# A two-layer hybrid trunk step: norm and projection of each tile right behind its combination, and a last norm split between ScalarE and VectorE

## What is computed

```python
for l in range(2):
    h = x * (1 + sc_a) + sh_a
    qa, ka, va, oa, ia, fa, qb, kb, vb, qc, kc, vc = split_proj(h @ w_in[l])
    ya, yb, yc = mlstm(...), windowed_attention(...), neighbourhood_attention(...)
    x = post_norm(x, concat(ya, yb, yc) @ w_out[l], g_a, ln_g[l, 0], ln_b[l, 0])
    h = x * (1 + sc_f) + sh_f
    x = post_norm(x, moe_ffn(h, ...), g_f, ln_g[l, 1], ln_b[l, 1])

def post_norm(x, y, gate, g, b):
    u = ALPHA * x + gate * y
    mu = mean(u); var = mean((u - mu) ** 2)
    return (u - mu) * rsqrt(var + 1e-5) * g + b
```

## Time and profile before

| | us |
|---|---|
| median of 3 runs | 1696.19 (1695.11 to 1696.98) |
| the profiled execution, its own time | 1693.52 |
| its span | 1691.7 |
| TensorE busy | 1452.2 (86%) |
| VectorE busy | 625.5 (37%) |
| ScalarE busy | 344.0 (20%) |
| GpSimd busy | 404.6 (24%) |
| mean granted clock of TensorE, of full speed | 0.925 |

### The profile page before, as it was taken

The page is one execution under the profiler, slowest core; times in us unless marked ns, Lnnn a source line. Parts: engine busy times, 40 slices in busy tenths (PEclk is TensorE's granted clock), DMA queues, the critical chain, the costliest instruction groups (busy, mean ns, idle before and its releaser), DMA issues.

```text
span 1691.7 us, 23077 instructions
## 1 busy us (share of the span) xinstructions
PE 1452.2 (86%) x8501; PEld 998.0 (59%) x8501; DVE 625.5 (37%) x1470; ACT 344.0 (20%) x886; POOL 404.6 (24%) x541
## 2 busy tenths in 40 slices
PE   6999999997993899987699999999679479899772
PEld 4888998665882333332378988967468433334220
DVE  2201332864467121111520133376537732122127
ACT  2111112653010111110231111156401011111001
POOL 1000043522623112111110002352265221112113
PEclk8999999999995999998899999999799679899886
DMA  9311103775129899997512111275130779999951
GB/s 368 97 60 60 58 33 108 270 261 215 41 90 360 360 372 419 410 397 292 231 45 67 56 61 55 71 259 213 40 123 38 322 290 382 418 396 419 400 205 62
DMA packets 75758, 356.26 MB, mean 211 GB/s; under 512 B 21152, under 2 KB 24480, under 8 KB 40832
## 3 DMA queue, kind: packets, MB, share of 16 engines
q1 hardware_dynamic: 41184, 291.58, 43.8%
q0 software_dynamic: 21888, 48.83, 8.2%
q10 hardware_dynamic: 12576, 14.37, 2.5%
HBM read 344.37 MB, written 33.12 MB: 223 GB/s over the span
## 4 chain that ended last, share of the span: by engine, by line
PE 67%; DMA 19%; DVE 8%; issue 2%; POOL 2%; ACT 1%; SPq 1%; ACTq 0%; POOLq 0%; DVEq 0%
PE bank L974 24%; DMA att<-h_rows,cur 11%; PE bank L1317 11%; PE bank L1202 7%; PE bank L1336 4%; DMA ring<-in_w_exp 3%; PE bank L1301 2%; PE bank L723 2%; PE bank L1128 2%; DMA att<-bias_full 2%; PE bank L1102 1%; DMA z<-in_w_ada 1%; PE bank L931 1%; PE bank L738 1%; PE bank L1224 1%
## 5 line engine op out<-in xcount | busy, mean ns | idle before, releaser
L974 PE MATMUL bank<-ring,hT 128*128 128x256 f32 (+1 forms) x1920 | 411.3, 374 | 8.4 <-ACT hT L1441 4.4
L974 PEld LDWEIGHTS bank<-ring,hT 128*128 128x128 f32 x1920 | 353.3, 191 | 53.9 <-issue 9.4
L1317 PE MATMUL bank<-ring,att 128*64 128x512 f32 (+1 forms) x448 | 188.4, 653 | 3.7 <-DMA z<-in_w_exp 3.7
L1317 PE MATMUL bank<-z,att 128*64 128x512 f32 (+1 forms) x416 | 167.2, 626 | 16.6 <-DMA ring<-in_w_exp 16.6
L1202 PE MATMUL bank<-ring,hT 128*128 128x256 f32 x640 | 145.2, 386 | 7.1 <-DMA ring<-in_w_out 5.6
L1202 PEld LDWEIGHTS bank<-ring,hT 128*128 128x128 f32 x640 | 122.6, 194 | 23.9 <-issue 7.3
L2339 DVE TENSOR_TENSOR att<-att,bank 128x256 f32<-128x256 f32 x38 | 16.0, 421 | 295.4 <-ACT att L1671 295.4
L1317 PEld LDWEIGHTS bank<-ring,att 128*64 128x64 f32 (+1 forms) x448 | 61.2, 164 | 84.4 <-issue 82.6
L1317 PEld LDWEIGHTS bank<-z,att 128*64 128x64 f32 (+1 forms) x416 | 53.1, 152 | 76.2 <-issue 76.2
L2621 POOL COPY cur<-att 128x1 int32<-128x1 int32 (+1 forms) x38 | 6.9, 182 | 379.7 <-ACT att L1678 280.9
L1301 PE MATMUL bank<-const,att 128*128 128x128 f32 x320 | 48.5, 301 | 54.7 <-DMA att<-h_rows,cur 54.6
(11 more groups left out here) (362 smaller groups left out, 2185.3 us busy)
## 6 DMA issues: line engine op xcount, KB each, us to landing
...
```

The lines of the kernel that those rows point to most:

```text
L974: last = eng.matmul(bk[:, i * UN:i * UN + nw], hTv[:, k, t * P:(t + 1) * P], w[:, k, 0:nw], start=(k == 0), stop=(k == KD - 1))
L1317: last = eng.matmul(bank[2 + j][c * m_:(c + 1) * m_, :], e["xT"][:, j, k * P + c * m_:k * P + (c + 1) * m_], wv[c][:, :, k, :], start=(k = ...
```

## The change

Between the layers, TensorE's order changes. Tile 0 is turned behind tile 2's combination, as before; tiles 3 and 4 are combined before tile 1 is turned; tiles 2, 3 and 4 are turned each behind the projection of one tile, and the waits for the copied-out banks are taken tile by tile instead of piece by piece. ScalarE norms and copies strictly tile by tile (before, the norms ran two tiles ahead), and the second half of tile 3, like that of tile 4, is copied out by VectorE. On VectorE, `ln_nm` of the previous tile stands between the two halves of a combination instead of behind the statistics.

At the end, ScalarE does the statistics of every tile: a copy of the tile with a running sum, the sum times -1/1024 (minus the mean), the square of x minus the mean with a running sum, and that times 1/1024 plus 1e-5. The copies' outputs go to a place nobody reads. GpSimd still raises to -0.5. VectorE does scale and shift of every tile with two 1024-wide scalar-tensor-tensor operations, (x - mean) * ln_g and the result * root + ln_b, two tiles behind its combinations. GpSimd's `ln_shift` is gone there.

The diff, without the line that names the new steps for the semaphores:

```diff
@@ -313,6 +313,10 @@
 
         n = self.n - 1
         return self.ev.event(f"bank_full{n % BANKS}", ("full", n))
+
+    def fill(self, ins, *key):
+
+        ins.then_inc(*self.filled_as(*key))
 
     def filled_as(self, *key):
 
@@ -951,35 +955,33 @@
                 if l > 0:
                     for t in range(NT):
                         combined(l - 1, t)
-                        if t >= 2:
-                            turned_rows(t - 2)
+                        if t == 2:
+                            turned_rows(0)
+                    turned_rows(1)
                 for idx, n in enumerate(IN_ORDER):
                     w = unit_view((l, "in", n))
                     nw = min(UN, D_IN - n * UN)
                     for g in range(3):
                         bk = jobs.open("Z", l, n, g)
                         eng.wait_ge(*jobs.room())
-                        if l > 0 and idx == 0:
-                            for t in range(2 * g, min(2 * g + 2, NT)):
-                                for j in range(2):
-                                    eng.wait_ge(*jobs.empty("H", l, t, j))
                         if l == 0 and idx == 0 and g < 2:
                             for who in ("act", "dve"):
                                 eng.wait_ge(*ev.at("hmod", who, 2 * g))
                         for i, t in enumerate(range(2 * g, min(2 * g + 2, NT))):
+                            if l > 0 and idx == 0:
+                                for j in range(2):
+                                    eng.wait_ge(*jobs.empty("H", l, t, j))
                             if l == 0 and idx == 0 and t == 1:
                                 for who in ("act", "dve"):
                                     eng.wait_ge(*ev.at("hmod", who, 1))
                             for k in range(KD):
                                 last = eng.matmul(bk[:, i * UN:i * UN + nw], hTv[:, k, t * P:(t + 1) * P],
                                                   w[:, k, 0:nw], start=(k == 0), stop=(k == KD - 1))
-                        last.then_inc(*jobs.filled())
-                        if l > 0 and idx == 0 and g < 2:
-                            for t in ((2, 3), (4,))[g]:
-                                if t > 2:
-                                    turned_rows(t)
+                            if l > 0 and idx == 0 and t < NT - 2:
+                                turned_rows(t + 2)
+                        jobs.fill(last, "Z", l, n, g)
                         if g == 2:
-                            ev.table[("unit_used", l, "in", n)] = ev.table[("full", jobs.n - 1)]
+                            ev.table[("unit_used", l, "in", n)] = ev.table[("full", jobs.number(("Z", l, n, g)))]
                         if (l, idx, g) == (0, 0, 1):
                             bk = jobs.open("LNT")
                             eng.wait_ge(*jobs.room())
@@ -1450,16 +1452,13 @@
                     eng.activation(out, src, ACT.Copy).then_inc(*jobs.freed("Z", l, n, g))
 
                 if l > 0:
-                    ln_hat(2, 0, l - 1)
-                    ln_hat(2, 1, l - 1)
                     for t in range(NT):
+                        ln_hat(2, t, l - 1)
                         if t == NT - 1:
                             eng.wait_ge(*ev.at("comb", l - 1, NT - 1))
                             evac_z(IN_ORDER[0], 0)
-                        for j in range(2 if t < NT - 1 else 1):
+                        for j in range(2 if t < NT - 2 else 1):
                             evac_h(t, j)
-                        if t + 2 < NT:
-                            ln_hat(2, t + 2, l - 1)
                 g2 = region(small, 160, P, NT, 8)
 
                 def gate_logs():
@@ -1694,8 +1693,17 @@
                         rows = slice((k * NT + t) * P, (k * NT + t + 1) * P)
                         eng.dma_start(o12[:, t, k, :], y_dram[l][rows, :]).then_inc(*act.event("ld_o", l, t, k, by=16, sem=f"ld_o{t}"))
                 if l == DEPTH - 1:
-                    for t in range(NT - 1):
-                        ln_hat(2, t, l)
+                    for t in range(NT):
+                        junk = o12[:, t, 1, :]
+                        eng.wait_ge(*ev.at("comb", l, t))
+                        eng.activation(junk, x[:, t, :], ACT.Copy, accum_out=lnv[:, t, 0:1]).then_inc(*act.event("lnsum", l, t))
+                        eng.wait_ge(*act.last())
+                        eng.activation(lnv[:, t, 4:5], lnv[:, t, 0:1], ACT.Copy, scale=-1.0 / D).then_inc(*act.event("lnneg", l, t))
+                        eng.wait_ge(*act.last())
+                        eng.activation(junk, x[:, t, :], ACT.Square, bias=lnv[:, t, 4:5],
+                                       accum_out=lnv[:, t, 1:2]).then_inc(*act.event("lnsq", l, t))
+                        eng.wait_ge(*act.last())
+                        eng.activation(lnv[:, t, 2:3], lnv[:, t, 1:2], ACT.Copy, bias=EPS, scale=1.0 / D).then_inc(*act.event("lnvar", 2, l, t))
 
 
         @block.vector
@@ -1766,13 +1774,13 @@
                     eng.tensor_copy(lnT[:, :], bk[:, 0:64]).then_inc(*jobs.freed("LNT"))
                     eng.wait_ge(*jobs.empty("LNT"))
                 else:
-                    t = NT - 1
-                    bk = jobs.bank("H", l, t, 1)
-                    eng.wait_ge(*jobs.full("H", l, t, 1))
-                    for k in range(4, KD):
-                        last = eng.tensor_scalar(hTv[:, k, t * P:(t + 1) * P], bk[:, (k - 4) * P:(k - 3) * P], hgain[:, 1, k:k + 1],
-                                                 hshift[:, 1, k:k + 1], ALU.mult, ALU.add)
-                    last.then_inc(*jobs.freed("H", l, t, 1))
+                    for t in range(NT - 2, NT):
+                        bk = jobs.bank("H", l, t, 1)
+                        eng.wait_ge(*jobs.full("H", l, t, 1))
+                        for k in range(4, KD):
+                            last = eng.tensor_scalar(hTv[:, k, t * P:(t + 1) * P], bk[:, (k - 4) * P:(k - 3) * P], hgain[:, 1, k:k + 1],
+                                                     hshift[:, 1, k:k + 1], ALU.mult, ALU.add)
+                        last.then_inc(*jobs.freed("H", l, t, 1))
                 g1, g2 = region(small, 120, P, NT, 8), region(small, 160, P, NT, 8)
                 h4 = lambda ap: ap.rearrange("p (h n) -> p h n", h=HA)
 
@@ -2381,26 +2389,32 @@
                         eng.scalar_tensor_tensor(out=x[:, t, cols], in0=x[:, t, cols], scalar=ALPHA, in1=part, op0=ALU.mult,
                                                  op1=ALU.add).then_inc(*(dve.event("comb", l, t) if half else dve.step()))
                         eng.wait_ge(*dve.last())
-
-                end = l == DEPTH - 1
-                for t in range(NT):
-                    combine(t)
-                    ln_stats(2, t)
-                    if t > 0:
-                        ln_nm(2, t - 1)
-                    if end and t > 1:
-                        ln_gain(2, t - 2, m["lnend"], l)
-                if not end:
+                        if l < DEPTH - 1 and half == 0 and t > 0:
+                            ln_nm(2, t - 1)
+
+                def finish(t):
+                    part = o12[:, t, 0, :]
+                    eng.wait_ge(*ev.at("lnneg", l, t))
+                    eng.wait_ge(*ev.at("ld_ln", 2, l))
+                    eng.scalar_tensor_tensor(out=part, in0=x[:, t, :], scalar=lnv[:, t, 4:5], in1=m["lnend"][:, 0, :],
+                                             op0=ALU.add, op1=ALU.mult).then_inc(*dve.step())
+                    eng.wait_ge(*dve.last())
+                    eng.wait_ge(*ev.at("lnrstd", 2, l, t))
+                    eng.scalar_tensor_tensor(out=x[:, t, :], in0=part, scalar=lnv[:, t, 3:4], in1=m["lnend"][:, 1, :],
+                                             op0=ALU.mult, op1=ALU.add).then_inc(*dve.event("x2", l, t))
+
+                if l < DEPTH - 1:
+                    for t in range(NT):
+                        combine(t)
+                        ln_stats(2, t)
                     ln_nm(2, NT - 1)
                 else:
-                    t = NT - 1
-                    ln_gain(2, t - 1, m["lnend"], l)
-                    eng.scalar_tensor_tensor(out=x[:, t, :], in0=x[:, t, :], scalar=lnv[:, t, 0:1], in1=m["lnend"][:, 0, :],
-                                             op0=ALU.subtract, op1=ALU.mult).then_inc(*dve.step())
-                    eng.wait_ge(*dve.last())
-                    eng.wait_ge(*ev.at("lnrstd", 2, l, t))
-                    eng.scalar_tensor_tensor(out=x[:, t, :], in0=x[:, t, :], scalar=lnv[:, t, 3:4], in1=m["lnend"][:, 1, :],
-                                             op0=ALU.mult, op1=ALU.add).then_inc(*dve.event("x2", l, t))
+                    for t in range(NT):
+                        combine(t)
+                        if t >= 2:
+                            finish(t - 2)
+                    for t in range(NT - 2, NT):
+                        finish(t)
 
 
         @block.gpsimd
@@ -2647,10 +2661,6 @@
```

(4 more changed lines are left out.)

2 lines of the change are left out of this document (1 added, 1 removed).

## The result

| | before | changed |
|---|---|---|
| median of 4 runs, us | 1695.65 (1695.05 to 1696.98) | 1668.99 (1667.84 to 1670.89) |
| ratio to before | | 0.9852, 95% interval 0.9839 to 0.9865 |
| span of the profiled execution | 1691.7 | 1666.0 |
| TensorE's start of combining layer 0 | 818.05 | 816.70 |
| from there to the first gates matmul ("passage") | 59.01 | 49.21 |

The rows of the table add up to the difference of the spans: 1.35 + 9.80 + 1.51 + 10.49 + 2.55 = 25.7 us.

What follows compares the result with a forecast made beforehand. VectorE was taken to decide only in places, in the chain between the layers (with ScalarE's copies) and at the end, TensorE holding two thirds of the span; 1696.2 less 20.5 (10.1 passage, 10.4 end) gave 1675.7, range 1672 to 1682.

Steps and rivals of the forecast that it cites:

- The passage: 10.1 forecast: Between the layers: the first unit's projection done at 859.9 instead of 870.06, a gain of 10.1 us.
- ScalarE did not become the limit: Rival, between the layers: ScalarE becomes the limit, the passage gives 6 to 8 us, 1678 to 1680; chance 0.12.
- nothing was given back: Rival, behind the passage: a wait of gates or weights takes its gain back, leaving 1685.8; chance 0.05.
- the clock did not stay low: Rival, passage: TensorE's clock stays at its lower level, passage ends 19.2 us later, 1705 in all; chance 0.03.
- The end: 10.4 forecast: End of the kernel: VectorE's last operation moves from 1681.9 to 1671.5, a gain of 10.4 us.
- The one price not in the trace: At the end: an undisturbed 1024-wide STT on VectorE, taken as 1.22 us and 1.25 to the next start.
- An estimate by the rule: Rival, at the end: half-rate STTs, about 2.4 us each, end 1.6 us later than before, 1687.7; chance 0.03.
- ten STTs that the prediction calls added: At the end: ten 1024-wide scalar-tensor-tensor operations counted as added to VectorE for scale and shift.
- the store tail stays: Behind VectorE's last operation: the 9.8 us to the span's end, read as stores and close, stay unchanged.
- what the holes cost: TensorE between the layers: four holes counted at 8.4 us, and 1.8 us for two tiles' projection at lower clock.
- theory A: Follow-up forecast, passage alone: the parts add, 10 us faster (9.5 to 11); the shorter tail belongs to the end.
- rival C: Follow-up forecast, passage alone: what follows starts in a better state, 12 to 14 us faster, stretch between under 760.5.

Runs made afterwards that it cites:

- e7: The changed kernel with three useless 1024-wide GpSimd additions behind the power steps of tiles 1 to 3 at the end; one execution, 1671.79 us.
- e10: The kernel before with 72 useless matmuls on TensorE ahead of each layer's first combined tile; 1703.89 us, ratio 1.0052.
- e5: The changed kernel with the last tile's power step taken from GpSimd (ScalarE square root, VectorE reciprocal); 1665.80 us, ratio 0.9835.
- e6: The changed kernel with one more small GpSimd power step that waits for VectorE's last operation; one execution, 1674.23 us.
- e3: The kernel before, unchanged, for a second profile; one execution, 1691.88 us.
- e2: The kernel before with only the end changed, the passage's order as before; 1682.86 us, ratio 0.9913.
- e1: The changed kernel with the end as before, so only the passage is changed; 1682.11 us, ratio 0.9912.
- e4: The changed kernel, unchanged, for a second profile; one execution, 1670.35 us.
- e15: The kernel of e5 with the last tile's final operation and store in two halves of 512 columns; 1664.67 us, ratio 0.9813.
- e17: The kernel of e15 timed on the same chip as e16; 1666.55 us, ratio 0.9830.
- e16: The changed kernel, unchanged, timed on the same chip as e17 and the kernel before; 1670.36 us, ratio 0.9855.

## Why the prediction was right and where it failed

*The passage: 10.1 forecast, 9.8 in the profile.* The closeness is in part luck: 10.7 behind the first 24 matmuls, less 0.9 because these ran slower in this execution (over all profiles of both orders without useless matmuls ahead of them they take 11.9 to 13.6). Norm 0 started 3.5 us earlier (827.61 against 831.12; 1.35 of it is the earlier start, so against the first combination it is 2.2, not the 3 expected, for the same reason), TensorE's new waits are two of 0.32 us, ScalarE's copies take 2.90 and its norms 1.24, and the gates' chain moved along: its last VectorE step at 863.79, its reader at 865.91, the same 2.1 us. ScalarE did not become the limit, nothing was given back, and the clock did not stay low; those rivals fell.

*The end: 10.4 forecast, 10.5 in the profile.* The one price not in the trace was right from its lower bound: an STT of 1024 is 1.28 us, and a tile's two take 1.32 and 1.20 to the next start, 2.52 for the 2.5 taken. An estimate by the rule of the Trainium skill's Vector Engine (DVE) Microarchitecture Reference, section 7, gives about 2.4 for one; the rows disagree. That the slow STTs came from GpSimd's additions is shown by e7. ScalarE took 2.9 us a tile for the 3.3 taken. Two of the ten STTs that the prediction calls added stood there before (tile 4's); the sum goes forward from the new order and does not need their number. That forecast and profile agree to 0.1 is luck too: TensorE's 40 combining matmuls there take 18.8 to 20.4 us, and with them the end varies from 42.3 to 43.8 us in the profiles with the old end and from 32.0 to 33.0 in those with the changed one (e10, with useless matmuls ahead, left out).

*The step that failed: "the store tail stays".* The 9.8 us behind VectorE's last operation were read as stores and close and carried over. They are GpSimd's drain, counted from GpSimd's last operation (e5, e6). The change moves that operation against VectorE's last one from 1.07 us ahead (1680.82, 1681.89) to 3.43 ahead (1655.31, 1658.74), and the tail shrinks by 2.5. My own numbers held it: tile 4's root ready at 1668.0 and VectorE done at 1671.5 are the same 3.5 us apart.

*The second, a term mis-sized: what the holes cost.* I counted 8.4 us of holes and one slow place (8.83 for 7.07), 1.8 us, as the one profile showed, and took that profile for the median. In the old order the number of such places varies: one in that profile and in e3, three in e2 (64.02), two in e10. Nine profiles of the new order (the changed kernel, e1, e4 to e7, e15 to e17) show none, 48.3 to 49.4 us. Filling the holes alone was worth 3.6 us in the medians (by the ratio 4.7, with its interval 2.5 to 6.8), for the 1.8 that I had in the sum. At 1.7 us a place that is two to three slow places in a run, an estimate. The order itself, with no slow place on either side, gives 45.40 - 36.37 = 9.0 us. With the 3.6 that is 12.6, and e1 took 14.0 off the median (by its ratio 14.9, 12.0 to 17.8): this clock accounts for e1's surplus over theory A, and no run shows what rival C gave as its reason.

Together: 20.5 forecast, plus 2.5 of tail, plus 1.8 of clock, is 24.8 of the 26.7 us, and inside the 22.9 to 27.3 of the ratio. On e16's chip the medians are 24.6 apart (1694.95, 1670.36). The rest is no larger than the scatter of the stretch between, and I assign it to nothing. The two parts timed alone add up to 27.3 us (14.0 and 13.3), at the upper edge of that interval.
